# Row factors as a diagonal in the turning products, convolution moved ahead of the query norms, and chunk sums on VectorE, in a decoder layer on one core

## The reference, cut to what matters

```
h = rms_norm(x, ln_mix_g)
a_q, a_k, a_v, b_a, b_g, c_q, c_kv, c_kr, d_u = split(h @ w_in)
o = concat[ local attention(a_*) | convolution(b_*) | latent attention(c_*) | state space model(d_u) ]
x = x + group_norm(o) @ w_out
x = x + cross_attention(rms_norm(x), rms_norm(mem))
x = x + experts(rms_norm(x))

rms_norm(x, g) = x * rsqrt(mean(x * x) + 1e-6) * g
convolution: z = a * sigmoid(g); 31 taps along the tokens + bias; layer_norm over 512 features; silu; @ pw_w + pw_b
```

## Time and profile before

| what | value |
|---|---|
| device time, median of 3 runs | 1506.9 us (1505.21 to 1511.48) |
| device time of the profiled execution | 1509.87 us |
| its span | 1507.9 us |
| mean granted TensorE clock | 0.909 of full |
| PE busy | 1181.2 us, 78% |
| DVE busy | 559.5 us, 37% |
| ACT busy | 206.4 us, 14% |
| DMA engines, mean rate | 318 GB/s |

### The profile page before, as it was taken

How to read it: one execution, slowest core, us unless ns; L and a number is a source line. 1 busy time by engine, 2 the same in 40 slices (tenths; PEclk the granted TensorE clock), 3 DMA queues, 4 the chain that set the end, 5 groups by cost and what they waited for, 6 DMA issues and landing times.

```text
span 1507.9 us, 19372 instructions
## 1 busy us (share of the span) xinstructions
PE 1181.2 (78%) x8383; PEld 577.9 (38%) x8383; DVE 559.5 (37%) x1232; ACT 206.4 (14%) x440; POOL 13.9 (1%) x31
## 2 busy tenths in 40 slices
PE   5999999998999998867656775776677577657766
PEld 4885564666444553322222332222222222222222
DVE  3887759875002334312322131222123122212222
ACT  3202010364001331100000000010000000100000
POOL 3000000000000000000000000000000000000000
PEclk9999999999999998988987898899788888988988
DMA  9432453420335576999999999999999999999996
GB/s 304 152 140 92 173 195 133 173 71 28 112 120 215 202 276 254 428 427 427 429 426 427 428 426 427 427 426 428 427 427 427 427 428 427 426 428 427 426 429 267
DMA packets 72803, 480.07 MB, mean 318 GB/s; under 512 B 14677, under 2 KB 20949, under 8 KB 44688
## 3 DMA queue, kind: packets, MB, share of 16 engines
q1 hardware_dynamic: 71696, 477.96, 77.2%
q0 software_dynamic: 864, 0.25, 0.2%
q10 hardware_dynamic: 160, 0.64, 0.1%
HBM read 476.71 MB, written 2.11 MB: 318 GB/s over the span
## 4 chain that ended last, share of the span: by engine, by line
PE 49%; DMA 41%; DVE 4%; ACT 4%; issue 1%; SPq 0%; DVEq 0%; ACTq 0%
DMA ring<-in_moe_w_up_dram 24%; DMA late_ring<-in_moe_w_up_dram 13%; PE bank L613 9%; PE bank L1039 9%; PE bank L875 7%; PE bank L634 6%; PE bank L1005 3%; DMA late_ring<-in_moe_w_down_dram 3%; PE bank L1071 3%; PE bank L1084 2%; PE bank L935 2%; PE bank L597 1%; PE bank L901 1%; DMA x_tok<-in_x_dram 1%; ACT hT L1205 1%
## 5 line engine op out<-in xcount | busy, mean ns | idle before, releaser
L1039 PE MATMUL bank<-ring,x_gathered 128*32 128x256 f32 x2720 | 294.4, 436 | 138.0 <-DMA late_ring<-in_moe_w_up_dram 71.0
L2132 DVE TENSOR_TENSOR tokens_out<-tokens_out,bank 128x512 f32<-128x512 f32 x240 | 148.7, 681 | 449.0 <-PE bank L1084 449.0
L1039 PE MATMUL bank<-late_ring,x_gathered 128*32 128x256 f32 x1376 | 199.8, 442 | 76.1 <-DMA ring<-in_moe_w_up_dram 75.0
L1039 PEld LDWEIGHTS bank<-ring,x_gathered 128*32 128x32 f32 x2720 | 133.9, 123 | 263.6 <-issue 229.2
L613 PE MATMUL bank<-ring,hT 128*128 128x512 f32 (+2 forms) x416 | 156.2, 536 | 3.9 <-ACT hT L1205 2.2
L1039 PEld LDWEIGHTS bank<-late_ring,x_gathered 128*32 128x32 f32 x1376 | 87.5, 125 | 139.2 <-issue 124.0
L1005 PE MATMUL bank<-x_tok,select 128*32 128x512 f32 x512 | 115.9, 1032 | 6.1 <-DVE select L2161 3.2
L875 PE MATMUL bank<-ring,oT 128*128 128x512 f32 x256 | 110.2, 592 | 0.0
L613 PEld LDWEIGHTS bank<-ring,hT 128*128 128x128 f32 x416 | 78.5, 190 | 80.2 <-issue 67.4
L1071 PE MATMUL bank<-ring,hidden 128*32 128x512 f32 x656 | 77.2, 597 | 21.4 <-DVE hidden L2124 21.2
L2088 DVE TENSOR_TENSOR x_gathered<-bank,gain_cols 128x512 f32<-128x512 f32 x32 | 22.1, 691 | 180.7 <-PE bank L1024 180.7
(11 more groups left out here) (388 smaller groups left out, 984.9 us busy)
## 6 DMA issues: line engine op xcount, KB each, us to landing
ring<-in_moe_w_up_dram SPq DMA_DIRECT2D x41, 2048.0 KB, 33.6
ring<-in_moe_w_gate_dram SPq DMA_DIRECT2D x40, 2048.0 KB, 38.4
ring<-in_moe_w_down_dram SPq DMA_DIRECT2D x39, 2048.0 KB, 34.3
late_ring<-in_moe_w_down_dram SPq DMA_DIRECT2D x21, 2048.0 KB, 33.5
late_ring<-in_moe_w_gate_dram SPq DMA_DIRECT2D x20, 2048.0 KB, 37.9
late_ring<-in_moe_w_up_dram SPq DMA_DIRECT2D x20, 2048.0 KB, 33.7
ring<-in_w_in_dram SPq DMA_DIRECT2D x20, 1024.0 KB, 9.8
ring<-in_w_out_dram SPq DMA_DIRECT2D x16, 1024.0 KB, 7.4
```

The source lines that it names most:

```text
L1039: mm = pe.matmul(gu_bank[SLOTS * c:SLOTS * c + SLOTS, 0:256], XGT[:, at, k % 4, k // 4, :], pieces[c // 2][:, a:a + 256], start=k == 0, st ...
L2132: ins = v.tensor_tensor(y, x, mix[c][:, :], ALU.add)
```

## The change

Four things change together.

1. The first turning. PE multiplies the raw tile of x by a diagonal matrix that holds the tokens' row factors (`token_diagonal`), so that turning and scaling are one fp32 product (64 MATMUL records in place of 32 transposes). DVE drains the eight tasks and multiplies by the gain, which now lies as 128x16 columns, loaded by ACT's queue (`drain_gained`). The gain's load of 1 MB by SP is gone. The row factor comes from ACT's Sqrt (with a load of its function table), a reciprocal and one correcting step. Three small loads of the state space model go to ACT's queue too.
2. The convolution stands on DVE ahead of the local queries' norm, and accumulates in `knT` (as `CV`). Its sums cm and cv stand on PE among the memory products.
3. Five of the six sums over features: DVE adds the four chunks first (`feature_sum`, a reduction that reads with a step of 256 elements), and PE does one product with ones (`row_sum`). gs2 stays as it was.
4. Orders. Latent queries stand ahead of the gated product, the latent keys ahead of pw; gs3 and gs1 later; the local output of the second tile ahead of the latent one; on DVE the weights of the local window are normalised ahead of the latent maximum; and SP loads the bias band after the piece pw and not between two pieces of xk.

```diff
@@ start @@
-            sp.dma_start(GB[:, :], inp["ln_mix_g"].to_broadcast([P, D])).then_inc(s["gain_in"], 16)
+            act.dma_start(GM[:, :], inp["ln_mix_g"][0].rearrange("(p k) -> p k", k=KD)).then_inc(s["gain_in"], 16)
             act.dma_start(K[:, :], const_d).then_inc(s["const_in"], 16)
@@ tensor @@
-                model_transposes("xT", tt, xn_of[tt])
+                x = X[:, tt, :].rearrange("p (f k) -> p k f", k=KD)
+                for q in range(4):
+                    b = fill(f"xT{tt}{q}")
+                    for i in range(4):
+                        mm = pe.matmul(b[:, P * i:P * i + P], x[:, 4 * q + i, :], DG[:, tt, :], start=True, stop=True)
+                    filled(mm)
@@ scalar @@
+            for tt in range(TT):
+                act.wait_ge(s[f"x_in{tt}"], 16)
+                mean_square(X[:, tt, :], xn_of[tt], 144 + tt, "mean_sq")
+                if tt == 0:
+                    act.wait_ge(s["const_in"], 16)
+                st.link(nc.scalar.activation(SM[:, 272 + tt:273 + tt], SM[:, 144 + tt:145 + tt], ACT.Sqrt, scale=1.0,
+                                             bias=const("eps")), "root")
@@ vector @@
+            def token_diagonal(tt):
+                dve.wait_ge(s["mean_sq"], tt + 1)
+                a, y, w = SM[:, 160:161], SM[:, 176:177], SM[:, 192:193]
+                st.sent(v.tensor_scalar(a, SM[:, 144 + tt:145 + tt], EPS, None, ALU.add))
+                dve.wait_ge(s["root"], tt + 1)
+                link(v.reciprocal(y, SM[:, 272 + tt:273 + tt]))
+                link(v.tensor_scalar(w, y, y, a, ALU.mult, ALU.mult))
+                link(v.scalar_tensor_tensor(y, w, -3.0, y, ALU.add, ALU.mult))
+                link(v.tensor_scalar(DG[:, tt, :], ident, y, -0.5, ALU.mult, ALU.mult), "xn")
+            token_diagonal(0)
+            drain_gained(0, 0)
+            drain_gained(0, 1)
+            token_diagonal(1)
+            for tt, q in ((0, 2), (0, 3), (1, 0), (1, 1), (1, 2), (1, 3)):
+                drain_gained(tt, q)
@@ vector, sums @@
+            def feature_sum(dst, src, sem):
+                link(v.tensor_reduce(dst, src.rearrange("p k t -> p t k"), AX.X, ALU.add), sem)
@@ tensor, sums @@
+            def row_sum(name, src):
+                filled(pe.matmul(fill(name, cols=T), const("ones"), src, start=True, stop=True))
+            memory_product("xv", 0)
+            memory_product("xv", 1)
+            pe.wait_ge(s["conv_sum"], 1)
+            row_sum("cm", RG[:, 1, :])
+            memory_product("xk", 0)
+            pe.wait_ge(s["conv_sq"], 1)
+            row_sum("cv", RG[:, 0, :])
+            memory_product("xk", 1)
@@ vector, end of the attentions @@
             wait_task(dve, "sl13")
             window_maximum(1, SL1)
+            group_scale(1)
+            window_normalise(1, SL1)
             wait_task(dve, "ml0")
             latent_maximum(0, latent[0])
-            window_normalise(1, SL1)
             latent_normalise(0)
             wait_task(dve, "ml11")
             latent_maximum(1, latent[1])
             latent_normalise(1)
             wait_task(dve, "so1")
-            group_square(0, SQ0)
+            group_square(0, SQ0, SUM0)
```

More of the change, by code:

```diff
@@ L119, in task_order @@
     t += [f"mT{tt}{q}" for tt in range(TT) for q in range(4)]
-    t += ["xv0", "xv1", "xk0", "xk1", "cqT0", "cqT1", "ckvT", "glu0", "cm", "glu1"]
-    t += ["mq00", "cv", "mq01", "gs3", "mq10", "mq11", "pw0", "pw1", "mkv00", "mkv01", "mkv10", "mkv11"]
-    t += ["sqT0", "sqT1", "skT", "gs1", "sl00", "sl01", "sl10", "sl11", "sl12", "sl13", "sp00", "sp01"]
+    t += ["xv0", "xv1", "cm", "xk0", "cv", "xk1", "cqT0", "cqT1", "ckvT"]
+    t += ["mq00", "mq01", "mq10", "mq11", "glu0", "glu1", "mkv00", "mkv01", "mkv10", "mkv11", "pw0", "pw1"]
+    t += ["gs3", "sqT0", "sqT1", "skT", "sl00", "sl01", "gs1", "sl10", "sl11", "sl12", "sl13", "sp00", "sp01"]
     t += ["qnT0", "qnT1", "qrT0", "qrT1", "knT0", "knT1", "krT", "so0", "ml0", "ml10", "ml11"]
-    t += ["sp10", "sp11", "sp12", "sp13", "mp0", "kxT0", "kxT1", "mo0", "so1", "mp10", "mp11", "gs0", "mo1", "gs2"]
+    t += ["sp10", "sp11", "sp12", "sp13", "mp0", "kxT0", "kxT1", "so1", "mo0", "mp10", "mp11", "gs0", "mo1", "gs2"]
     t += [f"wo{n}{tt}" for n in range(4) for tt in range(TT)]
@@ L254, in trunk @@
         RG = sb("conv_rows", [P, 2, T], stack=front)
+        GM = sb("mix_gain_cols", [P, KD], stack=front)
         BL = sb("ssm_b_lhs", [P, 2, 4, P], stack=front)
@@ L298, in trunk @@
         SQ2 = KNT
+        CV = KNT[:, :, :]
+        DG = RG[:, :, 0:P]
+        SQ3 = XN[:, 0:1024].rearrange("p (k t) -> p k t", k=GC)
+        SUM3, SUM1, SUM0 = XN[:, 1024:1280], XN[:, 1280:1536], XN[:, 0:256]
         SQ0 = XN[:, 1024:2048].rearrange("p (k t) -> p k t", k=GC)
@@ L480, in _ @@
                     sp.dma_start(XNO, inp["mem"][0, P:T, :]).then_inc(s["mem1_in"], 16)
-                if key == ("xk", 2):
+                if key == ("pw", 0):
                     sp.wait_ge(s["dist_out"], 16)
@@ L775, in key_turned @@
                     transposes(f"{prefix}{tt}", src(tt), parts=parts)
+            wait_task(pe, "cqT1")
+            for tt in range(TT):
+                for g in range(2):
+                    latent_query(tt, g)
             pe.wait_ge(s["gelu"], 1)
             glu(0)
-            pe.wait_ge(s["conv_part"], GC * CONV_W)
-            column_sums("cm", OT[:, 4:8, :])
             glu(1)
[L782 to L793, removed]
             wait_task(pe, "ckvT")
@@ L797, in _ @@
                     latent_keys(tt, g)
+            pe.wait_ge(s["conv_z"], 1)
+            for i in range(2):
+                feature_major(f"pw{i}", [("pw", 0)], lambda k: ZT[:, k, :], 2 * i, GC)
+            pe.wait_ge(s["og_sq"], 1)
+            row_sum("gs3", SUM3)
             pe.wait_ge(s["sq_n"], 2)
@@ L807, in _ @@
                 window_scores(f"sl0{i}", 0, range(4 * i, 4 * i + 4))
+            pe.wait_ge(s["og_sq"], 2)
+            row_sum("gs1", SUM1)
             for i in range(4):
@@ L862, in _ @@
             pe.wait_ge(s["og_sq"], 3)
-            column_sums("gs0", SQ0)
+            row_sum("gs0", SUM0)
             wait_task(pe, "mp11")
@@ L1342, in _ @@
                                        for f in range(2)])
-            for tt in range(TT):
-                for g in range(2):
-                    drain(f"mkv{tt}{g}", MKV[:, tt, 512 * g:512 * g + 512])
+            root_mean_square("gs3", RG2[:, 3, :])
             for tt in range(TT):
```

165 lines of the change are left out of this document (82 added, 83 removed).

## The result

| | before | changed |
|---|---|---|
| device time, median of 20 runs each | 1507.0 us (1504.5 to 1515.1) | 1515.9 us (1507.6 to 1524.8) |
| ratio | | 1.0063, 95% interval 1.0043 to 1.0083 |
| profiled execution, its span | 1509.9, 1507.9 us | 1513.0, 1511.1 us |
| mean granted clock | 0.909 | 0.906 |

The forecast was 1499.3 us, with a range from 1492 to 1508. The 20 times of the changed kernel form two groups: eleven from 1507.6 to 1516.0 us with a mean clock of 0.902 to 0.908, and nine from 1520.6 to 1524.8 with 0.895 to 0.901. The profiled execution is of the first group.

The account below looks back on a forecast made before the run. The experts were taken as bound by their 12.6 MB loads, the layer ahead by PE, tied by SP's queue. Terms -0.6, -0.1, -3.9, +1.6, -4.6 sum to -7.6 us: 1502.3 profiled, 1499.3 against 1506.9, range 1492 to 1508.

Parts of the forecast that it names:

- start, to u0: Turning of x on PE: first record at about 12.3 us, u0 at 23.5, 0.6 us earlier than before.
- u0 to the latents' turns: Convolution 0; sums and xk -0.1 us, with fewer products on PE and xk's 0.99 us wait gone.
- middle: 272.05 to 317.56 us: sum products, conv_z's wait and its slow spell go, two new pauses come; -3.9 us.
- local scores: 317.56 to 330.83 us: gs1's product 0.4, slow spell behind the skT pause 1.8, wait of 0.57 covered; +1.6 us.
- attentions: 330.83 to 365.43 us: waits of 2.31 and 1.88 go, gs0 saves 1.3, new pause 2.2, one spell fewer; -4.6 us.
- If the first 16 alone are slow: PE's 64 turning records at the start: 9.4 us if only 16 run at half rate, 14.6 if all do.
- the start stays slow: Rival: all 64 turning records take 0.228 us, u0 at 27.9, 3.7 late; 1503.6 us; chance 0.12.
- I take 22 slow and 42 fast, 10.0 us: Time taken for PE's 64 turning records at the start, 22 at half rate and 42 at full rate.
- I take 1.8 us for each such spell at 1.2 GHz: On PE, a pause of about 2 us costs itself and some 1.8 us more through half clock behind it.
- slow-reduction rival: Five stepped feature sums on DVE: gain gone at 4.8 us each, 1515 us at 7.5; chance 0.05.
- Whatever PE wins ahead of that moves the stream: PE's gain ahead of the expert piece SP issues at 587.04 us moves loads and end by the same amount.
- nothing arrives: Rival: loads alone set the end, so the front's gain is lost; 1506.9 us; chance 0.11.

Follow-up runs that it names:

- Experiment 4: The changed kernel with 14 additional, unread 128x256 products on PE ahead of the turning; median 1515.4 us, ratio 1.0035 to before.
- 5: The changed kernel with the turning products reading 128 neighbouring columns of x in place of every sixteenth; one run, 1506.0 us.
- 6: The changed kernel with the turning products' weight operand read at steps of 1, 2, 4 and 8 elements; one run, 1520.8 us.
- 7: The kernel before with its transposes reading 128 neighbouring columns in place of every sixteenth; one run, 1508.9 us.
- experiment 3: The changed kernel with the constants' load issued ahead of the gain columns on ACT's queue; median 1520.8 us, ratio 1.0060 to before.
- Experiment 8: The changed kernel with six additional, unread products filling PE's pause ahead of the local scores; median 1508.0 us, ratio 0.9991 to before.
- 9: The changed kernel with before's start and the local queries' and keys' turns moved ahead of the latent queries; median 1498.1 us, ratio 0.9928 to before.
- 10: The changed kernel, new start included, with the local queries' and keys' turns moved ahead of the latent queries; median 1503.9 us, ratio 0.9965 to before.

## Why the prediction was wrong

It forecast 1502.3 us for the profiled execution, and that took 1513.0. Stage by stage, by the starts of PE's rows in the two profiles (the latents' turns at 271.89 and 274.79):

| stage | forecast | measured | missed by |
|---|---|---|---|
| start, to u0 | -0.6 | +4.3 | 4.9 |
| u0 to the latents' turns | -0.1 | -1.4 | -1.3 |
| middle | -3.9 | -6.0 | -2.1 |
| local scores | +1.6 | +4.7 | 3.1 |
| attentions | -4.6 | -3.1 | 1.5 |
| output product to SP's piece | 0 | +2.1 | 2.1 |
| from there to the end | 0 | +2.5 | 2.5 |

**The start: the step that failed first.** "If the first 16 alone are slow: 3.65 + 5.7 = 9.4 us; if all are: 14.6." All took the slow pace, u0 came after the 26 us that the prediction had named as a sign of being wrong, and the rival "the start stays slow" had the size (u0 at 27.9, measured 28.4) with 0.12. But it had it by luck, its cause was wrong as well: both took the slow pace for the clock's, and a transpose's record for the price of a product's. Experiment 4 and the change's own profile show 0.21 us at full clock, 5 and 6 show that the step of the weight operand (64 bytes in the change) sets it, 7 that a transpose hardly minds it. With a contiguous operand "I take 22 slow and 42 fast, 10.0 us" would have held (9.23). I had the warning at hand: the Trainium skill (SBUF — State Buffer, Door 1: The DMA port swizzle) says that accesses that go to a new 16-byte line pay, and I weighed it for VectorE's sums alone, where at most 0.70 us each is due to it, and not for the operand that PE loads. The row agrees in kind, not in its border: the Trainium skill lets 4 elements of 4 bytes go free, and 4 cost all of it here (0.234 us against 0.12). The late constants are a second term of the miss: PE's first record stands at 13.46 in place of 12.3, and experiment 3 takes back 0.87 of these 1.2 us.

**The local scores: "I take 1.8 us for each such spell at 1.2 GHz."** The place was right (pause 2.85, forecast 2.7), the size wrong: I took the two spells of the profile for what any pause costs. Here half clock lasted 10.2 us in the profile, and 27 in the two profiled long runs (experiments 4 and 6). Experiment 8 shows that the pause is the trigger; it is worth 5.0 us in the profile and 0.7% of the median, since the long runs go with it. With nine of twenty of those, the median is 2.9 above the profiled execution, while I had carried the 3.0 by which before's profile stood above its median.

**The middle** was right part by part: wait for xk, the conv_z wait and its spell gone, no wait at cm, pauses of 2.23 and 2.85. But the spell behind the first pause didn't come (1.8 too much), nor the one that before's profile has from 91.6 to 95.0 us, which the earlier trace rows didn't show in their means. That was luck of the profile: experiments 3, 4 and 6 have the same pause of 2.2 us and 3.4 us of half clock behind it, over products that take 12.1 to 12.3 us in place of 10.6. The convolution cost nothing.

**The attentions:** no pause ahead of sp1 and so1, and 2.42 ahead of mp0 (forecast 2.2). The one spell that the sum kept came behind gs0's pause (362.4 to 365.7 us) and not behind that. Gs0 waited 2.40 us where before it was 0.99, so 1.4 more and not 0.5; 0.7 of that is the stepped reduction, which the sum had at 1.22. The pause of 0.80 ahead of mp10 wasn't in the sum. The slow-reduction rival falls: 1.92 us, far from its 4.8.

**What ties front and end.** "Whatever PE wins ahead of that moves the stream" holds to the letter: in all thirteen profiles the stretch from SP's piece to the last landing is 898.6 to 899.4 us, with the piece anywhere from 572.6 to 599.0. The rival "nothing arrives" falls. But I priced what comes after the output product and behind the last landing at nothing, and both have clocks of their own: 2.1 and 2.7 us.

**Open** stays what decides between 10 and 27 us of half clock in the scores, and why the change falls into the long one in 9 runs of 20, the same middle on the old start in 2 of 12. The ratios say that this matters: the rest without the new start (0.9972) and the new start alone (1.0030) multiply to 1.0002, and the change has 1.0063, more than the intervals of the three allow. So with the pause left in, start and middle do not add up, and 0.6% is theirs together; with the pause filled (0.9991, experiment 8) or gone (experiments 9 and 10) they do. The long runs aren't all of it, since the eleven short ones have a median of 1513.0 us, 0.4% above before.

## What to carry to other kernels

Before a transpose is turned into a product, look at how its operand lies: a step that is free for a transpose can nearly double the time per record of a product (0.12 to 0.21 and more here). Price a new pause on PE by what followed such pauses in several profiles, not in one: here 2.2 us ahead of the latent queries cost nothing more in four profiles and about 1.7 us more in three, and 2.85 us ahead of the small products of the local scores cost 5 or 13 more. Whether the width of what follows or the length of the pause makes that difference was not separated. A transfer that PE waits for is best preceded by work that was due anyway, and if there is none, even by work that isn't.

## What the runs showed of the hardware

- A 128x128 weight load in fp32 products runs at a pace of 0.12 us per record with steps of 1 and 2 elements, and 0.21 to 0.24 with 4, 8 and 16, at full clock (experiments 4 to 6). At the start's slower rate it is 0.21 for 1 and 2, so there the step hides.
- Behind the last landing the rest of the span took 22.0 to 22.1 us in six of the thirteen profiles (before's among them), 23.3 in two and 24.6 to 24.8 in five (the change's among them), with the same instructions: the clock there is worth up to 2.8 us of every measurement. It goes with the pause in which PE waits for that landing: 2.4 to 3.2 us in the six, 4.2 to 4.9 in the other seven.
- A trace's record of the clock begins only some way into the kernel, and a window ahead of it says 1.00 whatever the rate is. In experiment 4 it begins at 4.9 us: the additional products of 128x256 pass at 3.30 / 8 = 0.41 us ahead of that and at 4.40 / 21 = 0.21 behind it, and both windows say 1.00. In before it begins at 23.3 us, behind both slow sets of transposes.

```profile
1.50:4.80 3.30, 3.30 (x8) 2.67 (x9) 0.00 (x0) 1.11 (x1) 3.30 (x7) 1.00 0.84 295
5.00:9.40 4.40, 4.40 (x21) 3.60 (x19) 0.00 (x0) 2.00 (x2) 4.40 (x10) 1.00 1.01 406
```
